# Three feed-forward layers with down units in three passes, modulation rows packed four to a tile, and another order of the first stage

## The reference, cut to what matters

```
m = (silu(c) @ w_mod[i] + b_mod[i]).reshape(b, 1, 9, d)     # shift, scale, gate of each sublayer
def half_ffn(x, g, shift, scale, gate, w13, w2):
    h = rms_norm(x, g) * (1 + scale) + shift
    a, b = split(h @ w13, 2)                                # w13: 1024 x 5632
    return x + 0.5 * gate * ((silu(a) * b) @ w2)            # w2: 2816 x 1024
```

## Time and profile before

| | us |
|---|---|
| median of three runs | 2507.69 |
| lowest, highest | 2500.26, 2511.84 |
| the profiled execution, its own time | 2501.64 |
| its span, first to last instruction | 2499.8 |
| PE busy in the span | 2397.4 (96%) |
| DVE busy | 1430.5 (57%) |
| ACT busy | 1000.5 (40%) |
| granted clock of TensorE, mean | 0.958 |
| moved by DMA | 535.45 MB, 214 GB/s |

### The profile page before, as it was taken

How to read it: one execution, slowest core, us unless ns; L and a number is a source line. 1 busy time by engine, 2 the same in 40 slices (tenths; PEclk the granted TensorE clock), 3 DMA queues, 4 the chain that set the end, 5 groups by cost and what they waited for, 6 DMA issues and landing times.

```text
span 2499.8 us, 35746 instructions
## 1 busy us (share of the span) xinstructions
PE 2397.4 (96%) x15358; PEld 2158.7 (86%) x15358; DVE 1430.5 (57%) x1609; ACT 1000.5 (40%) x1257; POOL 4.5 (0%) x12
## 2 busy tenths in 40 slices
PE   9999999989999999999999988899999899899997
PEld 7788888867998999888998986899998888899996
DVE  0875676323763465234652442688887433888886
ACT  2211132214330332042321323577776344676774
POOL 0000000000000000000000000000000000000000
PEclk8999999989999999999999988899999789899998
DMA  7456767522777477543775431488886332488884
GB/s 277 172 196 240 265 227 271 192 68 79 259 279 277 171 292 294 186 152 129 262 276 212 151 118 37 148 300 294 300 305 242 142 121 75 179 304 295 296 307 180
DMA packets 94195, 535.45 MB, mean 214 GB/s; under 512 B 9984, under 2 KB 12296, under 8 KB 46800
## 3 DMA queue, kind: packets, MB, share of 16 engines
q1 hardware_dynamic: 92480, 524.33, 58.3%
q0 software_dynamic: 816, 5.65, 0.6%
q10 hardware_dynamic: 736, 3.10, 0.3%
HBM read 531.97 MB, written 1.06 MB: 213 GB/s over the span
## 4 chain that ended last, share of the span: by engine, by line
PE 90%; DVE 6%; ACT 3%; issue 1%; DVEq 0%; ACTq 0%
PE PS L777 25%; PE PS L1231 12%; PE PS L850 9%; PE PS L888 8%; PE PS L1259 7%; PE PS L812 5%; PE PS L935 5%; DVE moe_low L2202 2%; PE PS L1199 2%; PE PS L733 2%; PE PS L699 2%; PE PS L1179 1%; PE PS L659 1%; PE PS L742 1%; PE PS L876 1%
## 5 line engine op out<-in xcount | busy, mean ns | idle before, releaser
L777 PE MATMUL PS<-h_parts,ring_low 128*128 128x256 f32 (+1 forms) x1408 | 440.0, 313 | 0.0
L777 PE MATMUL PS<-h_parts,g_parts 128*128 128x256 f32 x2112 | 383.0, 284 | 0.9 <-DVE h_parts L1813 0.9
L2202 DVE TENSOR_TENSOR moe_low<-moe_ring,W_HIGH 128x2048 fp32r<-128x2048 f32 x128 | 292.9, 2290 | 83.1 <-ACT W_HIGH L1615 83.1
L777 PEld LDWEIGHTS PS<-h_parts,g_parts 128*128 128x128 f32 x2112 | 328.9, 192 | 2.4 <-issue 1.2
L1231 PE MATMUL PS<-moe_low,HXH 128*96 128x256 f32 x1024 | 287.9, 281 | 0.0
L777 PEld LDWEIGHTS PS<-h_parts,ring_low 128*128 128x128 f32 x1408 | 269.9, 192 | 16.1
L1615 ACT ACTIVATE W_HIGH<-moe_ring 128x2048 fp32r<-128x2048 f32 x128 | 244.5, 1912 | 23.4 <-PE PS L1259 22.7
L850 PE MATMUL PS<-G,ring 128*128 128x256 f32 x1056 | 236.5, 385 | 2.8 <-DVE G L1898 2.8
L850 PEld LDWEIGHTS PS<-G,ring 128*128 128x128 f32 x1056 | 201.3, 192 | 30.7 <-DVE G L1898 3.4
L1460 ACT ACTIVATE SG<-PS 128x256 f32<-128x256 f32 (+1 forms) x88 | 38.4, 437 | 462.9 <-PE PS L777 462.9
L1231 PEld LDWEIGHTS PS<-moe_low,HXH 128*96 128x96 f32 x1024 | 166.2, 162 | 0.3
(11 more groups left out here) (316 smaller groups left out, 4653.6 us busy)
## 6 DMA issues: line engine op xcount, KB each, us to landing
moe_ring<-moe_w SPq DMA_DIRECT2D x192, 1024.0 KB, 4.9
CB<-mod_rows SPq DMA_DIRECT2D x200, 512.0 KB, 5.9
ring<-up_w SPq DMA_DIRECT2D x88, 1024.0 KB, 5.0
ring<-lin_w SPq DMA_DIRECT2D x55, 1024.0 KB, 4.9
ring<-down_w SPq DMA_DIRECT2D x24, 1408.0 KB, 6.0
CB<-mod_dual SPq DMA_DIRECT2D x24, 512.0 KB, 4.1
ring<-down_w SPq DMA_DIRECT2D x10, 1024.0 KB, 7.8
ring<-mod_w SPq DMA_DIRECT2D x8, 1024.0 KB, 7.0
```

The lines of the kernel that those rows point to most:

```text
L777: return mm(dst(h), a[:, k, h * P:(h + 1) * P], b[:, k, :], start=start, stop=(k == KT - 1 and j == 2), skip_group_check=True)
L2202: tt(by_tile(moe_low[:, moe_slot(l, p), :]), by_tile(moe_ring[:, moe_slot(l, p), :]), w_high_tiles(p), ALU.subtract).then_inc(w_low, 1)
```

## The change

Its parts:

1. **Feed-forwards 1 to 3.** `up` and `down` give way to `ffn(f)` with 33 units in the order of FFN_UNITS: four up units, then one down unit after each two up units, and two down units at the end. A down unit is now 1 MB: two tiles of inputs by all 8 tiles of outputs, 16 products by three passes, with ACT and DVE splitting the weight and the gated tile (GATED, GATED_HIGH, GATED_LOW). The 8 outputs add up in four PSUM banks over 11 down units.
2. **Modulation rows.** A tile of 128 partitions now holds 32 inputs of four rows of m instead of 128 inputs of one. Seven groups of 32 chunks replace 28 rows of 8 chunks. A chunk has the same 512 KB. PE sums a group with 8 products of four columns (16 for the first group). The feed-forwards hold 104, 40, 40 and 40 chunks.
3. **First stage.** DVE adds up the squares of the 8 tiles and PE needs four products for them. DVE multiplies X by the root (H0) while PE runs the last mod units, and scale and shift come after. `spare` runs 8 products instead of 14.
4. POOL loads the conditioning values in four transfers of 128 bytes a partition, and norms 3, 4 and 6 use another bank.

```diff
+ROWS, PARTS = 4, 32
+GROUP_CHUNKS = KT * P // PARTS
+N_GROUPS = (N_DUAL + N_ROWS) // ROWS
+FFN_UNITS = [("up", i) for i in range(4)]
+for _m in range(FT // 2 - 2):
+    FFN_UNITS += [("down", _m), ("up", 2 * _m + 4), ("up", 2 * _m + 5)]
+FFN_UNITS += [("down", FT // 2 - 2), ("down", FT // 2 - 1)]
 CHUNKS_AT = (
-    ([3] * 8 + [4] * 9 + [3] * 4 + [0], [4] * 5 + [2] + [4, 2] + [4] * 3 + [0]),
-    ([1, 1, 2] * 6 + [1, 1, 0, 0], [3, 2, 3, 2, 2, 2, 0, 0]),
...
+    ([3] * 10 + [2] + [4] * 8 + [0, 4, 0], [4] * 5 + [2, 4, 2, 0, 4, 4, 0]),
+    ([1] * 4 + [2, 1, 1] * 5 + [0, 1, 1] + [2, 1, 1] * 3 + [2, 0], []),
+    ([1] * 4 + [2, 1, 1] * 3 + [0, 1, 1] + [2, 1, 1] * 5 + [2, 0], []),
+    ([2] * 4 + [0, 1, 1] + [2, 1, 1] * 7 + [2] + [0] * 4, []),
 )
             def chunk_in(n):
-                src = mod_dual[n] if n < N_DUAL_CHUNKS else mod_rows[n - N_DUAL_CHUNKS]
+                g, k, part = n // GROUP_CHUNKS, n % GROUP_CHUNKS // ROWS, slice(n % ROWS * PARTS, (n % ROWS + 1) * PARTS)
                 if n >= 4:
                     sp.wait_ge(acc_steps, steps_after(n - 4))
-                sp.dma_start(ROWS_W[:, n % 4, :], src).then_inc(rows_full[n % 4], 16)
+
+                def put(j, rows, src):
+                    dst = ROWS_W[j * PARTS:(j + rows) * PARTS, n % 4, :]
+                    sp.dma_start(dst, src).then_inc(rows_full[n % 4], 16)
+                if g == 0:
+                    put(0, N_DUAL, mod_dual[k::KT, part, :])
+                    put(N_DUAL, 1, mod_rows[k:k + 1, part, :])
+                else:
+                    r0 = ROWS * (g - 1) + 1
+                    put(0, ROWS, mod_rows[r0 * KT + k:(r0 + ROWS - 1) * KT + k + 1:KT, part, :])
             def column_sums(g):
+                wait(pe, rows_taken, g)
+                for j in range(1 if g else 2):
+                    acc = ACC if g else DUAL_ACC[:, j, :]
+                    for d in range(KT):
+                        at = j * ROWS * KT + d
+                        last = mm(PS[:, GROUP_BANK[g], at:at + 3 * KT + 1:KT], acc[:, d * P:(d + 1) * P],
+                                  tab("block")[:, 0:ROWS], start=True, stop=True)
             def first_mods():
-                spare(10)
+                spare(8)
                     if i == 4:
                         pe.wait_ge(ld_rest, REST)
-                        for d in range(KT):
-                            mean_square(0, d)
+                        pe.wait_ge(sq_summed, KT - 1)
+                        for t in range(2 * TT):
+                            last = mm(PS[:, 7, t:t + 1], G[:, 0, t * P:(t + 1) * P], tab("mean1024")[:, 0:1],
+                                      start=True, stop=True)
+                        last.then_inc(ms_psum, 1)
+                    if i == 6:
+                        spread_roots(0)
+            def ffn(f):                                    # PE, a down unit
+                        def products(t, d):
+                            j = 2 * i + t
+                            pe.wait_ge(g_low, FT * f + j + 1)
+                            (bank, half), at = Y_BANK[d], j % 6
+                            pairs = ((high, GATED_HIGH), (high, GATED_LOW), (low, GATED_HIGH))
+            def norm0():                                   # DVE
+                for d in range(1, KT):
+                    tt(G[:, 0, :], G[:, 0, :], G[:, d, :], ALU.add).then_inc(sq_summed, 1)
+                dve.wait_ge(rb_psum, 1)
+                for d in range(KT):
+                    tt(H0[:, d, :], X[:, d, :], PS[:, 7, :], ALU.mult).then_inc(xn_ready, 1)
```

More of the change, by code:

```diff
@@ L84, in chunk_plan @@
         counts = list(ups_at) + list(downs_at)
-        steps = [dict(chunks=[], sums=[], dual=[], takes=[]) for _ in counts]
+        steps = [dict(chunks=[], sums=[], takes=[]) for _ in counts]
         for i, count in enumerate(counts):
@@ L852, in down @@
                     last.then_inc(unit_done, 1)
-                    if i:
-                        mean_square(AFTER_DOWN[f], i - 1)
-                    sums(f, FT + i)
+                    sums(f, n)
+                for d in range(2, KT - 1):
+                    mean_square(AFTER_DOWN[f], d)
                 keep_busy(AFTER_DOWN[f], 3)
@@ L1740, in _ @@
             pool.memset(eps[:, :], EPS).then_inc(eps_ready, 1)
+            for part in range(ROWS):
+                src = bass.AP(cols_in.tensor, part * PARTS * NCOLS, [[0, ROWS], [NCOLS, PARTS], [1, 4 * KT]])
+                pool.dma_start(cond_raw[:, part, :], src).then_inc(ld_cond, 16)
             pool.wait_ge(ext_ready, 3)
@@ L1888, in up, with rows_step, up0 @@
+            def rows_step(step):
+                for g in step["takes"]:
+                    take_group(g)
+                for n in step["chunks"]:
+                    add_chunk(n)
+            def up0():
                 for i in range(FT):
-                    step = PLAN[f][i]
-                    if i and (f == 0 or i + 1 < FT):
-                        split(f, i + 1)
-                    if f == 0 and i == FT - 1:
+                    if i:
+                        split(0, i + 1)
+                    if i == FT - 1:
@@ new lines, in up0, with ffn, gated_low @@
+                    tt(G[:, i, :], SG[:, i % 4, :], PS[:, 2 * (i % 2) + 1, :], ALU.mult).then_inc(g_ready, 1)
+                    rows_step(PLAN[0][i])
+            def ffn(f):
+                def gated_low(i):
+                    dve.wait_ge(g_high, FT * f + i + 1)
+                    tt(GATED_LOW[:, i % 6, :], GATED[:, i % 6, :], GATED_HIGH[:, i % 6, :], ALU.subtract).then_inc(g_low, 1)
+                units = len(FFN_UNITS)
+                for n, (kind, i) in enumerate(FFN_UNITS):
+                    if n + 2 < units:
+                        split(f, n + 2)
+                    else:
+                        split_next(f, n + 2 - units)
+                    if n and FFN_UNITS[n - 1][0] == "up":
+                        gated_low(FFN_UNITS[n - 1][1])
+                    if kind == "up":
+                        dve.wait_ge(silu_ready, FT * f + i + 1)
+                        tt(GATED[:, i % 6, :], SG[:, i % 4, 0:S], PS[:, i % 2, S:2 * S], ALU.mult).then_inc(g_ready, 1)
+                    if n == units - 2:
+                        gate_columns(f)
+                    rows_step(PLAN[f][n])
+                for d in range(KT):
+                    if d == KT - 1:
+                        dve.wait_ge(unit_done, UNIT0[f"ffn{f}"] + units)
+                    else:
+                        dve.wait_ge(y0_psum, 6 + 4 * (f - 1) + (1, 1, 2, 2, 3, 3, 4)[d])
+                    bank, half = Y_BANK[d]
+                    update(f, d, bank, half * S)
@@ L2309, in _ @@
             norm(5)
-            up(3)
-            down(3)
+            ffn(3)
             norm(6)
```

502 lines of the change are left out of this document (252 added, 250 removed).

## The result

The changed kernel takes 3152.07 us (median of 4 runs, 3144.29 to 3162.45) against 2507.15 before: ratio 1.2578, interval 1.2527 to 1.2628. It is slower, as forecast, but 252 us beyond the forecast and 62 beyond its range. The profiled execution took 3156.93 us.

What follows compares the result with a forecast made beforehand. PE bound the kernel before, with transfers next; four-engine chunks were to bound the feed-forwards. 177 + 10 + 63 + 68 + 82 - 6 = +394 on 2501.6 makes 2896, called 2900 for the median, range 2760 to 3090.

Steps and rivals of the forecast that it cites:

- Four engines for a chunk: Chunk transfers: 4 blocks of 32 rows are dealt over the same 4 of 16 DMA engines each time.
- 4.97 us for a chunk: Chunk transfers: 524,288 bytes on 4 engines at 26.4 GB/s each take 4.97 us, against 1.24 on all 16.
- The failed step: Feed-forwards: the chunk's four engines also carry a sixteenth of each weight unit, 2.5 us, or 3.1 for a down unit.
- 13 for gaps: Feed-forward 0: 13 us added for SP waiting on DVE to free a buffer while DVE waits for a unit.
- The slower rival: Chunk transfers: four engines at 21 GB/s each, 6.2 us a chunk, 240 us more, about 3140; chance 0.03.
- The 10 us for mixer A: After feed-forward 0: chunks left over delay mixer A's first weights, +10 us.
- The down units' runs: Feed-forwards 1 to 3: 1 KB runs make a down unit 3.1 us instead of 2.5, 7 us a feed-forward.
- What PE saves: Feed-forwards and row sums: three-pass down products save 39 us in three feed-forwards, row sums 38 us less.
- 2417 forecast: Whole kernel if all 16 engines carry a chunk and PE stays the bound: 2417 us; a rival, chance 0.16.
- The first stage: Before feed-forward 0: DVE adds the squares, so the first product comes at about 60 instead of 65.6, 6 us less.
- PE only waits longer for DVE: First stage: the two fewer spare products save nothing, as PE just waits longer for DVE.
- The range: Whole kernel: 2760 to 3090, reaching as far again past 2800 to 3000 (chunk 4.7 to 5.3 us, gaps 0 to 40).

Runs made afterwards that it cites:

- experiment 7: Whole-chunk kernel plus six series of loads alone at its end, varying blocks and partitions written: 392 GB/s for whole chunks, 248 for 16 blocks.
- experiment 8: Whole-chunk kernel plus six series of weight units and chunks at its end: three units alone 8.0 us, with four 4-block chunks 32.5 us.
- Experiment 3: Changed kernel with the down units of feed-forwards 1 to 3 laid out in 8 KB runs instead of 1 KB, chunks still in four blocks: 3158.29 us.
- experiment 9: Changed kernel with each chunk as one block of 128 rows and down units in 8 KB runs, both laid out by the host: 2403.07 us, ratio 0.9593.
- experiment 1: Changed kernel with each chunk laid out by the host as one tile of 128 rows of 4 KB, one transfer each: 2408.83 us, ratio 0.9634.

## Why the prediction was right in kind and wrong in size

- **Four engines for a chunk**: right. A share of 0.26 at 105 GB/s, and completions that fell by what four engines to a chunk makes. By the numbers it is also right that the count of the outer dimension decides: 4 blocks 105 GB/s, 8 blocks between, 16 or 32 all engines. That they are the lowest four and always the same was the Trainium skill's rule, and the records name no engines. That they are the same ones fits: where chunks alone follow one another (700 to 710, and experiment 7) the share is 0.26, which rotating ones would exceed.
- **4.97 us for a chunk**: right. 524,288 bytes at the steady 105 GB/s of experiment 7 are 5.0 us; I use 5.1 here.
- **The failed step** is the sentence "The four that a chunk loads also carry a sixteenth of each weight unit: 2.5 us for 1 MB at 418 GB/s" (and 3.1 for a down unit): it prices the two kinds one after the other, as if neither slowed the other. The mechanism of the forecast held, this term was too small. A unit beside chunks leaves 4.3 to 4.5 us in the kernel's steps, and 3.5 and 4.0 in experiment 8. With 4.5 and 5.1, feed-forward 0 gets 32 units by 2, 64 us, and 104 chunks by 0.13, another 14: 78, where 74 were missing (664 against 590, in which 13 for gaps were a guess). In the others 33 units by 1.6 (4.3 over the mean of 2.5 and 3.1) and 5 for the chunks make 58, where 64, 66 and 43 were missing. In feed-forward 3 that is 15 too many: its last four units have no chunk beside them, which explains 6, and the rest stays open.
- **The slower rival**, "each slower than in a full transfer", had the right direction and the wrong object: it priced the chunk up by 1.2 us, where a chunk alone takes its 5.0 and the pair is what grew, by some 2 us for each unit. That its 3140 lies 12 us from the measured time is luck.
- **The 10 us for mixer A** came, by another way than forecast. It isn't the mixer's weights that are late. DVE adds a left-over chunk that landed at 731.9 before it adds the first outputs to X, and the 24 records of the mean squares then take 5.28 us where they took 2.73 (the granted clock is 0.65 from 728.4 to 747.8).
- **The down units' runs**: the Trainium skill (DMA: Bandwidth & Descriptors, Specifications) puts line rate at 512 B and more; the store's row made them 7 us a feed-forward dearer. Experiment 3 saw no gain from longer runs, and experiment 9 none clear of its interval, so they speak for the Trainium skill here. A trace of the difference is left: with whole chunks, feed-forward 1's down units land after 5.8 us with 1 KB runs and after 5.2 with 8 KB.
- **What PE saves**: right, but shown only where the transfers let it: 2408.83 in experiment 1 for 2417 forecast, with 1.69 us for a row sum of four columns (forecast 1.68).
- **The first stage**: 2 us earlier, not 6. The store that DVE waits for lands at 29.7, as forecast. DVE's additions take 5.5 us (forecast 4.9) and the four sums 1.8 (1). PE stood still for 9.1 us ahead of the sums, and behind them two mod units take 9.96 us at a granted clock of 0.71, the next two 6.92 at 1.00; before, the four took 15.41 at 0.91. So they are 1.5 us longer, which "PE only waits longer for DVE" had left out. In experiment 1 the first product is at 63.57 too, so the chunks are not what holds it. The stretches of the two pairs:

```profile
37.40:47.30 9.90, 9.90 (x34) 8.24 (x35) 0.18 (x1) 2.63 (x4) 0.00 (x0) 0.71 0.23 70
48.30:55.10 6.80, 6.80 (x34) 6.00 (x33) 6.80 (x9) 1.91 (x1) 0.00 (x0) 1.00 0.77 267
```

- **The clock** has no term in the sum. It is at 0.81 in feed-forward 0 (0.97 in the stretch before, 1.00 with whole chunks from 64 to 437). The steps there are set by transfers, so it costs little; at the edges it costs the 1.5 us and the 2.6 us above, and I did not add up the rest.
- **The range** reached to 3090 by doubling a spread that had only the chunk's price and the gaps in it. It had no case in which two kinds of transfer slow each other, though the stretch at 273 GB/s and 0.75 invited the question: that is 22.8 GB/s for a busy engine (273 / 0.75 / 16), not 26.4.

## What to carry to other kernels

Write down for each transfer how many engines its outermost count allows, and where in SBUF each of them writes: here a transfer over four engines held up those behind it on the same queue (a unit landed after 18.6 us instead of 5.0), and both kinds together took longer than the sum of each alone. Before changing what is stored, try the order of the dimensions: 32 parts of 4 rows instead of 4 rows of 32 parts was worth 740 us here. And when a change forecasts a loss from one transfer's form, run it with that form undone, since the rest may be a gain (here 4%).

## What the runs showed of the hardware that was not expected

- A DMA share near 1 doesn't mean that 400 GB/s flow: 1.03 stood beside 248 GB/s, 0.49 (8 engines) beside 58.
- Eight engines that write to neighbouring partitions move 58 GB/s, 16 apart 92, 4 apart 186.
- SP's issue of one load grew from 0.4 to 4.8 us, and to 20.5 us for four chunks, while the chunks ahead of it were under way: SP then runs no further ahead. With whole chunks and as many units it is back at 0.43, so a long issue is a sign of transfers that back up.
- The packets under 512 B of two kernels that differ in one transfer's form tell how many engines carry it: 2208 fewer for 192 chunks on four engines and 32 on 3 and 16.
